# Routing of a hierarchical expert mixture: the last weighted copy of a round at the round's end, placing behind the first gate products, routing in two chains

## What the reference computes

```python
t = u.reshape(bsz * s, d)
g_logits = t @ w_group_router + b_group_router              # 4 groups
g_val, g_idx = lax.top_k(softmax(g_logits), 1)
e_logits = (t @ w_expert_router + b_expert_router).reshape(n_tok, 4, 8)
sel_logits = einsum("tge,tg->te", e_logits, one_hot(g_idx))  # the 8 experts of the chosen group
e_val, e_idx = lax.top_k(softmax(sel_logits), 2)
weights = g_val * e_val / sum(e_val)
for e in range(32):
    hid = silu(t @ w_gate[e]) * (t @ w_up[e])               # 1024 -> 256
    out = out + combine[:, e:e + 1] * (hid @ w_down[e])     # 256 -> 1024
```

## Time and profile before

| | us |
|---|---|
| median of 3 runs | 471.84 (470.42 to 473.53) |
| the profiled execution | 472.22 |
| its span, first to last instruction | 470.3 |
| PE busy in the span | 417.5 (89%) |
| VectorE busy | 238.2 (51%) |
| ScalarE busy | 190.6 (41%) |
| GpSimd busy | 158.7 (34%) |

### The profile page before, as it was taken

How to read it: one execution, slowest core, us unless ns; L and a number is a source line. 1 busy time by engine, 2 the same in 40 slices (tenths; PEclk the granted TensorE clock), 3 DMA queues, 4 the chain that set the end, 5 groups by cost and what they waited for, 6 DMA issues and landing times.

```text
span 470.3 us, 9043 instructions
## 1 busy us (share of the span) xinstructions
PE 417.5 (89%) x3582; PEld 339.3 (72%) x3582; DVE 238.2 (51%) x529; ACT 190.6 (41%) x281; POOL 158.7 (34%) x107
## 2 busy tenths in 40 slices
PE   7999999999998999999989999966806999958973
PEld 6999999998998999999967565543303565524841
DVE  3589999999999945784386112210100122101014
ACT  4774556749976769444254121120100121201004
POOL 7589888882999983008000000000000000000001
PEclk9999999999999999999999999997966999988998
DMA  8886778652655477559794999999999999999962
GB/s 273 280 266 202 277 277 278 225 180 91 180 193 168 145 268 276 194 191 377 302 417 173 403 424 403 379 423 414 418 422 419 420 420 422 421 419 422 415 244 90
DMA packets 58160, 143.52 MB, mean 305 GB/s; under 512 B 4820, under 2 KB 43740, under 8 KB 46856
## 3 DMA queue, kind: packets, MB, share of 16 engines
q1 hardware_dynamic: 58104, 142.96, 79.9%
q10 hardware_dynamic: 16, 0.00, 0.0%
HBM read 141.91 MB, written 1.05 MB: 304 GB/s over the span
## 4 chain that ended last, share of the span: by engine, by line
PE 61%; DMA 17%; SPq 14%; DVE 3%; issue 3%; ACT 1%; POOLq 0%; DVEq 0%
PE ps L1352 14%; PE ps L1354 14%; PE ps L1353 14%; SPq L435 9%; PE ps L1573 8%; DMA ring<-in_w_down 5%; DMA ring<-in_w_up 5%; DMA ring<-in_w_gate 4%; SPq L453 4%; PE ps L1615 3%; DMA ring<-in_w_in 2%; SPq L431 2%; PE ps L1549 2%; PE ps L1524 2%; PE ps L1343 2%
## 5 line engine op out<-in xcount | busy, mean ns | idle before, releaser
L595 POOL TENSOR_TENSOR ring_r<-ring,ring_r 128x1024 fp32r<-128x1024 f32 x58 | 146.4, 2555 | 59.3 <-ACT ring_r L641 59.3
L1352 PE MATMUL ps<-u_hi,ring_r 128*128 128x256 f32 x368 | 104.4, 284 | 1.4 <-ACT gateA L649 0.9
L1354 PE MATMUL ps<-u_hi,ring_r 128*128 128x256 f32 x368 | 104.1, 283 | 0.0
L1353 PE MATMUL ps<-u_lo,ring_r 128*128 128x256 f32 x368 | 103.2, 280 | 0.0
L1573 PE MATMUL ps<-ring,xslot 128*32 128x256 f32 (+1 forms) x832 | 71.3, 415 | 31.9 <-DMA ring<-in_w_gate 21.7
L965 DVE SCALAR_TENSOR_TENSOR ps<-cpad,par,ps 128x256 f32<-128x256 f32 x232 | 92.0, 480 | 1.1 <-ACT ps L668 1.1
L601 POOL TENSOR_TENSOR hres<-xslot,gfin 128x512 f32<-128x512 f32 x1 | 1.3, 1265 | 244.6 <-ACT xslot L871 244.6
L1573 PEld LDWEIGHTS ps<-ring,xslot 128*32 128x32 f32 (+1 forms) x832 | 40.3, 126 | 58.6 <-issue 36.1
L641 ACT ACTIVATE ring_r<-ring 128x2048 fp32r<-128x2048 f32 x35 | 66.8, 1910 | 18.5 <-DMA ring<-in_w_rnn_out 9.3
L1352 PEld LDWEIGHTS ps<-u_hi,ring_r 128*128 128x128 f32 x368 | 69.1, 188 | 2.1 <-ACT gateA L649 1.1
L1353 PEld LDWEIGHTS ps<-u_lo,ring_r 128*128 128x128 f32 x368 | 70.0, 190 | 0.0
(11 more groups left out here) (271 smaller groups left out, 725.8 us busy)
## 6 DMA issues: line engine op xcount, KB each, us to landing
ring<-in_w_gate SPq DMA_DIRECT2D x28, 1024.0 KB, 14.9
ring<-in_w_in SPq DMA_DIRECT2D x24, 1024.0 KB, 5.6
ring<-in_w_up SPq DMA_DIRECT2D x24, 1024.0 KB, 18.4
ring<-in_w_down SPq DMA_DIRECT2D x12, 1024.0 KB, 13.6
ring_high<-in_w_up SPq DMA_DIRECT2D x8, 1024.0 KB, 17.2
extra<-in_w_down SPq DMA_DIRECT2D x8, 1024.0 KB, 17.2
ring<-in_w_down SPq DMA_DIRECT2D x16, 512.0 KB, 17.8
ring<-in_w_rnn_out SPq DMA_DIRECT2D x4, 1024.0 KB, 5.0
```

Of the source, the lines that this page charges most:

```text
L595: gp.tensor_tensor(ring_r[:, MIX_SLOT + k % SEG, cols], ring[:, MIX_SLOT + k % SEG, cols], ring_r[:, HI_SLOT + k % SEG, cols].bitcast(F32) ...
L1352: pe.matmul(dst, w_hi(k), x_hi(k), start=(k == 0), stop=False)
L1353: pe.matmul(dst, w_hi(k), x_lo(k), start=False, stop=False)
L1354: last = pe.matmul(dst, w_lo(k), x_hi(k), start=False, stop=(k == KC - 1))
```

## The change

A constant `ROUND_COPIES` is 11: the nine weighted copies inside a round and the two halves of its last one. The round's last weighted copies and its scatters stand at the end of the loop body on ScalarE, VectorE and PE, and the first pair of a round has no scatter and no weighted copy. The two dummy products, the zeros in `selT` and `wslot`, and the extra one in the counts of `pe_down` and `dve_ws` go away. The three placing products become a function, called on PE behind the first gate products; they write to bank 5. On VectorE the selection of the first group and the two remaining quarters of `hn_low` stand ahead of the placing steps, and the normalizing of the weights ahead of the wait for the placing products. The routing is written as two chains, one for the experts of each group and one for the groups, with a wait only where a value is used; the best expert of each of the four groups is taken at once, and the mask is made per 128 tokens. `keep_warm` is called with 1, 2 and 1 where it was 5, 3 and 5. `FIXED` is 8 where it was 6, so the first two quads of experts stand in fixed places, and SP waits for the order only ahead of unit 12.

```diff
-FIXED = 6
-RANK_PLACES = [(0, 6), (20, 24), (6, 20), (24, 32)]
-NARROW_FIXED = slice(4, 6)
+FIXED = 8
+RANK_PLACES = [(0, 8), (20, 24), (8, 20), (24, 32)]
+NARROW_FIXED = slice(4, 8)
+ROUND_COPIES = BLOCKS + 1
...
+        order_ps = ps[0:1, 5, NE:2 * NE]
+        ranks_ps = ps[:, 5, 2 * NE:4 * NE]
+        rankT_ps = ps[0:NE, 5, 4 * NE:4 * NE + T]
...
-            sp.wait_ge(dve_order, 1)
             for n in range(RING, SPAN_UNITS):
-                experts = [placed(e) for e in unit_places(n)]
+                if n == FIXED_UNITS:
+                    sp.wait_ge(dve_order, 1)
+                experts = unit_places(n) if n < FIXED_UNITS else [placed(e) for e in unit_places(n)]
                 place_free(0, n)
                 load_unit(n, experts=experts)
...
-            link(gp.tensor_scalar(selT[:, :, :].rearrange("p a (b t) -> p (a b) t", b=TC),
-                                  bcast(ones[:, :].rearrange("p (a t) -> p a t", a=1), 1, 2 * TC),
-                                  0.0, None, ALU.mult))
-            gp.memset(wslot[:, :], 0.0).then_inc(dve_ws, 1)
-            gp.wait_ge(dve_ws, 1)
...
-                    if u == 0:
-                        act.wait_ge(dve_rankT, 1)
-                    weighted_hi(1, r * PAIRS + (pairs_done(2 * u) + 1), r * NE + (2 * pairs_done(2 * u) + 1))
+                    if u:
+                        weighted_hi(1, r * PAIRS + pairs_done(2 * u), r * NE + 2 * pairs_done(2 * u))
...
+                act.wait_ge(dve_ws, (r + 1) * NE)
+                for half in range(2):
+                    act.wait_ge((pe_down_half, pe_down)[half], (r + 1) * PAIRS)
+                    act.activation(y_hi[:, half * 512:(half + 1) * 512], ps[:, 6 + half, :], ACT.Copy,
+                                   scale=wslot[:, 1:2]).then_inc(act_yhi, 1)
             n_rounds = nc.snap(count, min_val=1, max_val=MAX_ROUNDS)
...
+            e = step(v.tensor_reduce(top_e, grouped(el), AX, ALU.max))
+            g = step(v.tensor_reduce(stat[:, 12:14], gl, AX, ALU.max))
+            v.wait_ge(dve_step, e)
+            e = step(v.tensor_tensor(grouped(is_top), grouped(el), per_group(top_e), ALU.is_equal))
+            v.wait_ge(dve_step, g)
             v.tensor_tensor(rt[:, 0, :, 0:NG], gl, bcast(col(12), 2, NG), ALU.subtract).then_inc(dve_route, 1)
-            first_of(rt[:, 2, :, 0:NG], gl, col(12), NG, 3)
-            link(v.tensor_scalar(rt[:, 3, :, 0:NG], rt[:, 2, :, 0:NG], -1.0, 1e30, ALU.add, ALU.mult))
-            e4 = rt[:, 4, :, :].rearrange("p t (g e) -> p (t g) e", g=NG)
             for tc in range(TC):
-                drop = bcast(rt[:, 3, tc, 0:NG].rearrange("p (g a) -> p g a", a=1), 2, PER_GROUP)
-                last = step(v.tensor_tensor(rt[:, 4, tc, :].rearrange("p (g e) -> p g e", g=NG),
-                                            logit[:, tc, NG:].rearrange("p (g e) -> p g e", g=NG),
-                                            drop, ALU.add))
-            v.wait_ge(dve_step, last)
-            link(v.tensor_reduce(stat[:, 12:14], rt[:, 4, :, :], AX, ALU.max))
-            first_of(rt[:, 5, :, :], rt[:, 4, :, :], col(12), NE, 6)
-            link(v.scalar_tensor_tensor(out=rt[:, 7, :, :], in0=rt[:, 5, :, :], scalar=-2e30,
-                                        in1=rt[:, 4, :, :], op0=ALU.mult, op1=ALU.add))
-            link(v.tensor_reduce(stat[:, 10:12], rt[:, 7, :, :], AX, ALU.max))
-            v.tensor_tensor(stat[:, 8:10], stat[:, 10:12], stat[:, 12:14], ALU.subtract).then_inc(dve_route, 1)
-            first_of(rt[:, 8, :, :], rt[:, 7, :, :], col(10), NE, 6)
-            v.tensor_tensor(mask[:, :, :], rt[:, 5, :, :], rt[:, 8, :, :], ALU.add).then_inc(dve_mask, 1)
+                g = step(v.scalar_tensor_tensor(out=q_g[:, tc, :], in0=gl[:, tc, :], scalar=stat[:, 12 + tc:13 + tc],
+                                                in1=desc[:, 0:NG], op0=ALU.is_equal, op1=ALU.mult))
+            v.wait_ge(dve_step, e)
+            e = step(v.tensor_tensor(grouped(q_e), grouped(is_top), order_in, ALU.mult))
+            v.wait_ge(dve_step, g)
+            g = step(v.tensor_reduce(stat[:, 14:16], q_g, AX, ALU.max))
+            v.wait_ge(dve_step, e)
+            e = step(v.tensor_reduce(top_q, grouped(q_e), AX, ALU.max))
+            v.wait_ge(dve_step, g)
+            for tc in range(TC):
+                g = step(v.tensor_scalar(drop[:, tc, :], q_g[:, tc, :], stat[:, 14 + tc:15 + tc], -1e30,
+                                         ALU.is_lt, ALU.mult))
+            v.wait_ge(dve_step, e)
+            e = step(v.tensor_tensor(grouped(first), grouped(q_e), per_group(top_q), ALU.is_equal))
+            v.wait_ge(dve_step, g)
+            g = step(v.tensor_tensor(grouped(kept), grouped(el), per_group(drop), ALU.add))
+            side = step(v.tensor_scalar(chosen, drop, 0.0, None, ALU.is_equal))
+            v.wait_ge(dve_step, g)
+            e = step(v.scalar_tensor_tensor(out=rest, in0=first, scalar=-2e30, in1=kept, op0=ALU.mult, op1=ALU.add))
+            v.wait_ge(dve_step, side)
+            step(v.tensor_tensor(grouped(first_in), grouped(first), per_group(chosen), ALU.mult))
+            v.wait_ge(dve_step, e)
+            e = step(v.tensor_reduce(stat[:, 10:12], rest, AX, ALU.max))
+            side = step(v.tensor_tensor(top_kept, top_e, drop, ALU.add))
+            v.wait_ge(dve_step, e)
+            for tc in range(TC):
+                e = step(v.scalar_tensor_tensor(out=q_2[:, tc, :], in0=rest[:, tc, :], scalar=stat[:, 10 + tc:11 + tc],
+                                                in1=desc[:, :], op0=ALU.is_equal, op1=ALU.mult))
+            v.wait_ge(dve_step, e)
+            e = step(v.tensor_reduce(stat[:, 12:14], q_2, AX, ALU.max))
+            side = step(v.tensor_reduce(stat[:, 14:16], top_kept, AX, ALU.max))
+            v.wait_ge(dve_step, e)
+            for tc in range(TC):
+                v.scalar_tensor_tensor(out=mask[:, tc, :], in0=q_2[:, tc, :], scalar=stat[:, 12 + tc:13 + tc],
+                                       in1=first_in[:, tc, :], op0=ALU.is_equal, op1=ALU.add).then_inc(dve_mask, 1)
+            for tc in range(TC):
+                step(v.tensor_scalar(second[:, tc, :], q_2[:, tc, :], stat[:, 12 + tc:13 + tc], None, ALU.is_equal))
+            v.wait_ge(dve_step, side)
+            v.tensor_tensor(stat[:, 8:10], stat[:, 10:12], stat[:, 14:16], ALU.subtract).then_inc(dve_route, 1)
             hn_low(1, 0)
...
+            fill_sel(0, rt[:, 9, :, :]).then_inc(dve_sel, 1)
+            hn_low(0, 1)
+            hn_low(1, 1)
...
+            v.wait_ge(pe_place, 1)
+            v.tensor_copy(order_e[:, :], order_ps).then_inc(dve_order, 1)
...
-                    weighted_lo(1, g * 2 + 1)
+                    if u:
+                        weighted_lo(1, r * ROUND_COPIES + 2 * u)
...
+                v.wait_ge(dve_ws, (r + 1) * NE)
+                for half in range(2):
+                    cols = slice(half * 512, (half + 1) * 512)
+                    v.wait_ge(act_yhi, r * ROUND_COPIES + (BLOCKS + half))
+                    v.scalar_tensor_tensor(out=y_lo[:, cols], in0=ps[:, 6 + half, :], scalar=wslot[:, 1:2],
+                                           in1=y_hi[:, cols].bitcast(F32), op0=ALU.mult, op1=ALU.subtract
+                                           ).then_inc(dve_ylo, 1)
+            v.wait_ge(pe_scat, n_rounds * (2 * ROUND_COPIES))
...
-            pe.wait_ge(gp_step, 17)
+            pe.wait_ge(gp_step, 16)
             pe.wait_ge(gp_place, 1)
-            for b in (6, 7):
-                last = pe.matmul(ps[:, b, :], selT[:, 0, 0:P], selT[:, :, :].rearrange("p a t -> p (a t)"),
-                                 start=True, stop=True, skip_group_check=True)
-            last.then_inc(pe_down, 1)
...
-            keep_warm(5)
-            pe.wait_ge(dve_mask, 1)
+            keep_warm(1)
+            pe.wait_ge(dve_mask, TC)
...
-            keep_warm(3)
+            keep_warm(2)
...
-            keep_warm(5)
-            pe.wait_ge(dve_place, 1)
-            pe.wait_ge(dve_rankT0, 1)
-            pe.matmul(ps[0:1, 7, T:T + NE], place_k[:, 0:1], place[:, 2, :], start=True, stop=True)
-            for tc in range(TC):
-                pe.matmul(ps[:, 7, T + NE + tc * NE:T + NE + (tc + 1) * NE], rankT0[:, tc * P:(tc + 1) * P],
-                          place[:, 2, :], start=True, stop=True)
-            pe.matmul(ps[0:NE, 7, 0:T], place[:, 2, :], rankT0[:, :], start=True, stop=True).then_inc(pe_place, 1)
+            keep_warm(1)
...
+            def place_ranks():
+                pe.wait_ge(dve_place, 1)
+                pe.wait_ge(dve_rankT0, 1)
+                pe.matmul(order_ps, place_k[:, 0:1], place[:, 2, :], start=True, stop=True)
+                for tc in range(TC):
+                    pe.matmul(ranks_ps[:, tc * NE:(tc + 1) * NE], rankT0[:, tc * P:(tc + 1) * P],
+                              place[:, 2, :], start=True, stop=True)
```

(24 more changed lines are left out.)

89 lines of the change are left out of this document (36 added, 53 removed).

## The result

The changed kernel takes 469.34 us (median of 20 runs, 466.33 to 474.88) against 472.17 for the kernel before beside it (20 runs, 468.27 to 474.08): a ratio of 0.9941, 95% interval 0.9917 to 0.9965. That is 2.8 us (by the interval 1.7 to 3.9), under one per cent, where 2.7 was forecast. One run of the changed kernel, 474.88, counts as slow and is not in the ratio. The profiled execution took 469.49 us, its span 467.7 against 470.3.

The account below looks back on a forecast made before the run. PE's chain from the routing up to about 295 us was taken to set the end: 2.4 - 0.25 + 0.75 = 2.9, less 0.2 for the loop exit, gives 2.7 us. Forecast 469.1 us, range 467.0 to 471.4.

Parts of the forecast that it names:

- What bounds the kernel: Whole kernel: PE, fed by VectorE's routing, decides up to 295 us; bringing first products forward moves the end one for one.
- the gather starts after 244: Sign of being wrong, at PE's gather: it was expected at about 242.9 us.
- Routing interleaved: VectorE's routing as two overlapping chains: mask complete 3.1 us after the start, low half at 3.4, 1.25 us earlier.
- Selection ahead of placing: VectorE and PE ahead of the gather: placing steps leave the path, so the gather starts 3.7 us earlier, routing gain included.
- Placing behind the gate: PE between gate and up: placing products add 1.3 us, leaving 2.4 of the 3.7 us at the end of up.
- Loop entry: VectorE entering its loop before the first weight columns: charged 0.25 us, bounds nothing to 0.75.
- Empty pair: First block without its two scatters: 0.75 us back on PE before the first down products, 0 at the least.
- Sum: All terms together: 2.9 us gained at the first down products less 0.2 gives 2.7 us, time 469.1 us.
- Exit: ACT and VectorE leaving the loop between last copy and final norm: charged 0.2 us, bounds 0 to 0.47.
- fetch at the exit: Rival at the loop exit: ACT and VectorE stop for instructions read from memory, 4.9 us longer, time 473.8; chance 0.05.
- Dummy products and keep-warm calls: PE ahead of the gather: removing them lengthens nothing on the path as long as the clock holds; taken at nothing.
- The clock as a rival: Rival at PE's gather: without keep-warm calls the clock drops to 1.2 GHz, costing 1.6 us, time 470.7; chance 0.07.

Follow-up runs that it names:

- again before: The kernel before, unchanged, run and traced a second time: 472.34 us; PE's clock was half in the residual copies.
- Routing alone: The kernel before with only the new two-chain routing, counts and the rest as they were: 470.95 us, ratio 0.9988.
- count read early: The changed kernel with VectorE's read of the round count moved ahead of its wait for the placing products: 469.33 us, ratio 0.995.
- placing put back: The changed kernel with placing again ahead of the selection on VectorE and ahead of the gather on PE: 472.1 us, ratio 1.0014.
- the first trace of after: The changed kernel's first profiled execution, with nothing further edited: 469.49 us.
- the second measurement: The changed kernel run once more, unedited, against the kernel before: 469.06 us, ratio 0.9952.

## Why the prediction was right, step by step

**What bounds the kernel.** Right. Issuing the tenth unit 1.25 or 5.2 us later moved the eighteenth by -0.36 and 0.33 us, as the first down products moved. And what the eighteenth unit gains reaches the end: over eleven traces it is issued anywhere from 55.13 to 60.11 us after the reduction, and the last products start 160.2 to 161.5 us behind it. "PE's 2.9 is what passes on" held in kind, at 2.3 to 2.4. The sign of being wrong "the gather starts after 244" came true by the clock of the trace, at 244.52, but only by the longer mixer; counted from the reduction the gather came at what would have been 243.2.

**Routing interleaved.** The mechanism holds, the size was 1.25 and measured 0.96. What runs longer than I laid it out are the pairs with one instruction for each 128 tokens: from their start to the next step it is 0.45 us (L1142), 0.33 (the mask, L1149) and 0.29 (L1152). The mask is issued in full at 3.33 after the first reduction, not 3.1, and the low half follows at 3.69, not 3.4.

**Selection ahead of placing.** 3.7 forecast, 3.4 measured at the gather; the difference is the routing's 0.3.

**Placing behind the gate.** 1.3 forecast. From gate start to the end of up it is now 8.46 us, before 7.06: 1.4. Hence 2.0 at the end of up.

**Loop entry.** 0.25 charged; from the end of up to the hidden product it is 1.02 us and was 0.80, so 0.22. Reading the count earlier took that away again.

**Empty pair.** 0.75 forecast, 0.51 measured (2.09 to 1.58 us from the hidden product to the first down product). I let the down products start when the transposed values were there; PE starts them 0.24 us later (the copy of the transposed values ends at 259.35, the products start at 259.59), so the scatter had held them up for that much less.

**Sum.** 3.40 - 1.40 - 0.22 + 0.51 = 2.29 at the first down product, against 2.9. The cleared buffers and the larger `FIXED`, put at nothing, were not tried by themselves; the steps add up without them.

**Exit.** 0.2 charged, 0 measured, and the rival "fetch at the exit" falls: ScalarE goes on 0.01 us after its last copy. The rule of the Trainium skill (page "Runtime: NRT & Kernel Launch", section "Instruction fetch mechanics"), that a branch out of the engine's window waits for a fetch, cost nothing that shows in this trace. Whether this exit is such a branch, no run shows.

**Dummy products and keep-warm calls, taken at nothing.** This is the step that was incomplete. At the full clock it is right: gather at 5.63 with them back. At the half clock they stand between late residual copies and the counts. Against again before the change then gains 11.32 - 5.96 = 5.4 us at the gather and not 3.4 (5.96 from the traces of the changed order with a fall there), but the fall in again before lasted longer. Routing alone, with the old calls and placing and a fall that ends before 240 us as in those traces, has its gather at 9.71 (its counts wait for PE, not for the new routing): 3.75 us. So with a like fall the step gives some 0.35 us, and what of the 5.4 is the longer fall's stays open; no trace of the changed order has one of that length.

**The clock as a rival.** I put the fall into the gather, and priced it at 1.6 us. My argument against it, that a wait of 2.23 us before the last products had left the clock at 1.00, does not hold from trace to trace: behind waits of 2.22 and 2.19 us it fell there in count read early and in routing alone. In the gather it came only with placing put back, at 1.5. In the changed kernel and its neighbours it came in three other places: in the residual copies, in kernels with and without the change; behind the first up products; in the last down products. Behind the up products it appeared in two of nine traces without filling there, at 1.7 us, and in none of five with it. That is too few to say that the filling prevents it. The Trainium skill, page "TensorE: Matmul & The Clock Gate", section "HAM oscillation — how this bites in real kernels", puts such falls down to long waits for loads between products. The fall behind the up products is not that case: the idle pieces ahead of it were 1.11 and 0.34 us, none of them a wait for a load, and the first trace of after had the same without a fall. What decides it stays open.

**Why the total fits better than its terms.** The trace's gain of 2.3 us at the eighteenth unit grew to 3.83 at the last products, because the stream of loads between the two took 162.75 us in the trace of before and 161.22 after. Eleven of the 13 traces in which it can be read have 160.2 to 161.5, before again 160.97; so 1.5 us of this are the first trace's own, as the mixer's 1.32 the other way are the second's. So the chain gives 2.3 us, as the second measurement does, and the first one's 2.8 is within its interval of that. Executions of before with a fall in the copies would add to it, and those of after with one behind the up products take away; how often each happens is open, since only profiled executions show it. That 2.8 lies within 0.1 of the forecast 2.7 is in part luck: the terms were some 0.6 too large, and the 0.2 charged for the exit offset some of it.

## What to carry to other kernels

Follow a gain along the one chain that the end waits for, step by step from a fixed event of the trace, and not from the span's start: two traces of one kernel differed by over a microsecond ahead of the change. Where an engine is filled with products that nobody reads, ask what stands behind them when the work ahead of them runs late. Here an early start of one load was worth nothing at the eighteenth unit, because the next units waited for the same products as before.

## What the runs showed of the hardware

PE's granted clock fell to 0.50 in some executions of a kernel and not in others, with the same instructions: in the residual copies (4.4 to 6.0 us instead of 3.6 to 3.7 for eight products), in the first down products (5.35 instead of 3.65) and, set beside the same products of other kernels of the study, in the last (2.8 and 3.2 instead of 1.92). Ahead of these stood idle pieces of 0.3 to 2.2 us, and the same pieces stood in traces without a fall (2.23 us ahead of the last products of before, which took 1.92); in "placing put back" the gather fell to half although PE had waited only 1.25 us in one piece ahead of it. Leaving a loop cost ScalarE no time that shows (0.01 us between its last copy and the table load). Entering one, VectorE spent 1.0 us between its last weight and its first column, of which the earlier read of the count took 0.2 off the path.
